# Start addresses of the weight products' operands, and the place of 256-column units in their ring slot

## The chip, the cores and the metric

The kernel runs on one core of a Trainium2 chip. The metric is the device time of one execution in microseconds (us). The engines named here are TensorE (PE; its weight loads are PEld), VectorE (DVE), ScalarE (ACT), GpSimd (POOL) and SyncE (SP, which here only issues loads and stores). SBUF is the on-chip memory of 128 partitions; an address below is a byte offset within a partition, the same in all partitions. PSUM is where PE writes its sums, in banks of 512 floats per partition.

## What is computed

Two transformer layers in a row on 256 tokens of width 1024, all in 32-bit floats. Cut to what matters:

```python
def first_block(x, ...):
    u = rms_norm(x, ln_pre_mix)
    proj = u @ w_in                       # 1024 -> 9232 columns
    q_a, k_a, v_a, qkv_b, z_b, b_b, a_b, gate_a, gate_b = split(proj)
    y_a = moba_attention(rope(q_a), rope(k_a), v_a)
    qkv_b = silu(causal_depthwise_conv(qkv_b, conv_w))
    y_b = rms_norm(gated_delta_rule(...)) * silu(z_b)
    merged = sigmoid(gate_a) * (y_a @ w_proj_a) + sigmoid(gate_b) * (y_b @ w_proj_b)
    h = x + rms_norm(merged @ w_out)
    f = rms_norm(h)
    h = h + rms_norm((silu(f @ w_ffn_gate) * (f @ w_ffn_up)) @ w_ffn_down)   # 2816 wide
    return h + sigmoid(h @ w_ple_gate) * rms_norm(p @ w_ple)

def second_block(x, mem, ...):
    mem_n = rmsnorm(mem)
    q, k, v, u = split(rmsnorm(x) @ w_in_2)
    mix = concat(diff_attention(q, k, v), causal_multiscale_pool(u) @ w_pool) @ w_out_2
    x = x + rmsnorm(mix)
    xq = rmsnorm(x) @ w_xq;  kv = mem_n @ w_xkv          # cross attention on mem
    x = x + rmsnorm(cross(xq, kv) @ w_xo)
    hf = rmsnorm(x)
    return x + rmsnorm((silu(hf @ w_gate) * (hf @ w_up)) @ w_down)           # 2816 wide
```

## The kernel before

**Split products.** Every weight product is made of three products of a rounded 32-bit type (fp32r): an operand x is held as xH, its rounded value, and xL, the rest, and x times w is xH wH + xH wL + xL wH. `split_mm` (lines 480 to 482) issues the three.

**Weight units.** All large weights pass through the chip in 294 units of 128 x 1024 floats. SP loads a unit into `raw`, a ring of 4 slots (line 448); ACT copies it rounded to `w_hi`, a ring of 6 slots (line 1192); POOL subtracts to make `w_lo`, also 6 slots, in two halves of 512 columns (line 469); PE then uses both. A unit is either rows of a wide matrix (128 rows by 1024 columns), or two or four blocks of 128 rows by 512 or 256 columns.

**Which operand is stationary.** `mm(dst, a, b)` loads a (128 columns) as the stationary operand and streams b as the moving one. In the trace's names the moving operand comes first: `L<-w_hi,uH` is weights moving over stationary uH.
- Column steps (`column_unit`) and row steps (`row_piece`): the activations are stationary, 512 columns of weights move. The stationary tile is uH/uL in nearly all steps, yH/yL in proj_a, hH/hL in the two down steps, mH/mL in xkv 2 and 3, pH/pL in the small ple product (`embed`). In the last ffn step (`("ffn", 1, 5)`, `("ffn", 2, 5)`) only 256 columns are left, so 256 columns of weights move.
- conv (lines 849 to 851) and `keys` (xkv 0 and 1, lines 739 to 741): 128 columns of weights are stationary, and the 256 tokens of uH/uL or of mH/mL move. Both have the same loops: over pairs of column tiles, the eight row blocks, and two tiles each. The small `ba` product (lines 822 to 824) has baH/baL, 16 columns, stationary, and uH/uL moving.

A conv or keys unit holds 24 products of 256 columns, a row or column unit 12 of 512.

**Order.** `SCHEDULE` lists the steps and each engine walks it in its own order with semaphores between. `w_lo_there` counts finished units, `w_used` units that PE has done with; ACT waits for `w_used` before it overwrites a slot, SP for `w_lo_there`. `FILLING` puts column units into gaps of the attention steps.

**Addresses.** `place` gives tiles out one after another and rounds sizes up to 32 bytes. The order is raw (16,384 bytes), w_hi and w_lo (24,576 each), uH and uL (8,192 each), table (1608 floats, 6,432 bytes), small (960 floats, 3,840 bytes), then from address Y on yH and yL, hH and hL at the same place, and from B on everything else, at whole or half KB from B (`big`). The first free byte of SBUF is 16,481.

Of the kernel before, what the change touches and what calls it, by code (L numbers as in the profile page):

```python
# [22 lines left out]
F32 = mybir.dt.float32  # L23
F32R = mybir.dt.float32r
# [5 lines left out]
P = 128  # L30
# [15 lines left out]
WINDOWS = (2, 4, 8, 16)  # L46
RAW, SPLIT = 4, 6
UNIT = 1024
KB = 1024
MAGIC = 1.5 * 2.0 ** 23  # L50
TWO_PI = (6.28125, 2029 / 2 ** 20, 2 * np.pi - 6.28125 - 2029 / 2 ** 20)
# [166 lines left out]
def build(nc, a, out, known):  # L218
# [4 lines left out]
    UNITS = weight_units(w)  # L223
# [7 lines left out]
    with ctx:  # L231
# [2 lines left out]


        base = -(-nc.sbuf_base // 32) * 32
        at = [base]

        def place(name, shape, dt=F32, offset=None):
            size = 4 * int(np.prod(shape[1:]))  # L240
            if offset is None:
                offset = at[0]
                at[0] += -(-size // 32) * 32
            return nc.alloc_sbuf_tensor_at(name, list(shape), dt, offset=offset)

        raw = place("raw", [P, RAW, UNIT])
        w_hi = place("w_hi", [P, SPLIT, UNIT], F32R)
        w_lo = place("w_lo", [P, SPLIT, UNIT], F32R)
        uH = place("uH", [P, KD, SEQ], F32R)
        uL = place("uL", [P, KD, SEQ], F32R)  # L250
        table = place("table", [P, 5 * P + 2 * NT * HD + ROPE2 + LEVELS * HALF])
        small = place("small", [P, 960])
        Y = at[0]
        yH = place("yH", [P, KD, SEQ], F32R)
        yL = place("yL", [P, KD, SEQ], F32R)
# [155 lines left out]
        w_hi_there, w_lo_there, w_used = sem("w_hi_there"), sem("w_lo_there"), sem("w_used")  # L411
# [51 lines left out]
        @block.gpsimd  # L463
        def _(pool):
            for n in range(len(UNITS)):
                pool.wait_ge(w_hi_there, n + 1)
                for half in range(2):
                    cc = slice(half * UNIT // 2, (half + 1) * UNIT // 2)
                    last = nc.gpsimd.tensor_tensor(w_lo[:, n % SPLIT, cc], raw[:, n % RAW, cc], w_hi[:, n % SPLIT, cc].bitcast(F32),  # L469
                                                   ALU.subtract)  # L470
                last.then_inc(w_lo_there, 1)

# [2 lines left out]
        def _(pe):  # L475
# [6 lines left out]
                return mm(dst, sL, wH, start=False, stop=stop)  # L482

            def unit(n, k):
                slot = n % SPLIT
                return (w_hi[:, slot, :].rearrange("p (k n) -> p k n", k=k),
                        w_lo[:, slot, :].rearrange("p (k n) -> p k n", k=k))

            def column_unit(step, j, banks, n=512, sH=uH, sL=uL, tiles=range(NT), ks=None):

# [316 lines left out]
            for step in SCHEDULE:  # L807
                kind = step[0]
                if kind == "u":
                    n = CONV * 24 + KD  # L810
# [7 lines left out]
                elif kind == "ba":  # L818

                    pe.wait_ge(*VE(("u",), "split"))  # L820
                    for k in range(KD):
                        mm(Q[0][0:16, 0:SEQ], baH[:, k, :], uH[:, k, :], start=k == 0, stop=False)
                        mm(Q[0][0:16, 0:SEQ], baH[:, k, :], uL[:, k, :], start=False, stop=False)
                        last = mm(Q[0][0:16, 0:SEQ], baL[:, k, :], uH[:, k, :], start=False, stop=k == KD - 1)
                    last.then_inc(*PE.mark(step))
                elif kind == "rates":
                    pe.wait_ge(*VE(("ba",), "turned"))
                    for t in range(NT):
                        last = turn(Q[1][:, t * 16:t * 16 + 16], baT[0:16, t * P:(t + 1) * P], ident[0:16, 0:16])
                    last.then_inc(*PE.mark(step))  # L830
                elif kind == "conv":
# [7 lines left out]
                    for pair in range(2):  # L839
                        for k in range(KD):  # L840
# [5 lines left out]
                            for ct in (pair, pair + 2):  # L846
# [4 lines left out]
                                last = mm(bank, sL, uH[:, k, :], start=False, stop=k == KD - 1)  # L851
                            if pair == 1 and k % 2 == 1:
                                last.then_inc(w_used, 1)
                elif kind == "tok":
                    gr = step[1]
                    for part in range(3):
                        for t in range(NT):
# [8 lines left out]
                            for i in range(GH):  # L866
                                last = turn(Q[b % 3][:, i * P:(i + 1) * P], C[:, part * GH + i, t * P:(t + 1) * P], ident)
# [3 lines left out]
                elif kind == "decay":  # L871
# [6 lines left out]
                    for t in range(NT):  # L878
                        last = mm(Q[3][:, t * 8:t * 8 + GH], tri, g[:, t * 8 + gr * GH:t * 8 + gr * GH + GH], start=True, stop=True)
# [6 lines left out]
                elif kind == "feat":  # L886
# [6 lines left out]
                    for b, (what, t) in enumerate(lots):  # L893
# [5 lines left out]
                        for i in range(GH):  # L899
                            last = turn(Q[b % 3][:, i * P:(i + 1) * P], src[what](t, i), ident)  # L900
# [4 lines left out]
                    for t in range(NT):  # L905
                        for i in range(GH):
                            last = mm(Q[2 * t + i // 2][:, (i % 2) * 256:(i % 2 + 1) * 256], kT[:, t, i, :],
                                      kbqT[:, t, i, :, :].rearrange("p a b -> p (a b)"), start=True, stop=True)
# [3 lines left out]
                elif kind == "att":  # L912
                    gr = step[1]
                    for b in range(4):
# [3 lines left out]
                        for i in range(2):  # L918
                            for t in range(NT):
                                last = turn(Q[b][:, i * SEQ + t * P:i * SEQ + (t + 1) * P], mtok[:, part, t, 2 * pair + i, :], ident)  # L920
# [3 lines left out]
                    for i in range(GH):  # L924
                        last = mm(Q[0][:, i * P:(i + 1) * P], qTa[:, i, 0:P], kTa[:, i, 0:P], start=True, stop=True)
                    last.then_inc(*PE.mark(step, "scores", 0))
                    for i in range(GH):
                        last = mm(Q[1 + i // 2][:, (i % 2) * SEQ:(i % 2 + 1) * SEQ], qTa[:, i, P:SEQ], kTa[:, i, :], start=True, stop=True)
# [4 lines left out]
                    for b, j in enumerate((0, 1, 2)):  # L933
# [3 lines left out]
                        for i in range(GH):  # L937
                            last = turn(Q[b][:, i * P:(i + 1) * P], pr[:, i, j * P:(j + 1) * P], ident)
# [4 lines left out]
                    for i in range(GH):  # L943
                        bank = Q[3 if i < 2 else 0]
                        c0 = (i % 2) * SEQ
                        mm(bank[:, c0:c0 + SEQ], mtok[:, 2, 0, i, :], prT[:, i, 0:SEQ], start=True, stop=False)
                        last = mm(bank[:, c0 + P:c0 + SEQ], mtok[:, 2, 1, i, :], prT[:, i, SEQ:3 * P], start=False, stop=True)
# [4 lines left out]
                elif kind == "inv":  # L952
# [18 lines left out]
                    for l in range(1, LEVELS):  # L971
                        A = [Q[2], Q[3], Q[0], Q[1]] if l % 2 else Q
                        top = l == LEVELS - 1
                        for t in range(NT):
                            pe.wait_ge(*(VE(step, "T", l - 1, t) if l > 1 else AC(step, "T", 0, t)))
                            for i in range(GH):
                                for b, d in enumerate(diagonal):
                                    if top and b == 0:
                                        continue
                                    k = diagonal[0] if top else d  # L980
                                    last = mm(tiles(A[t], i)[b], AT[k, t, i, d], T[k, t, i, :], start=True, stop=True)  # L981
# [5 lines left out]
                        for t in range(NT):  # L987
# [3 lines left out]
                            for i in range(GH):  # L991
                                if top:
                                    d = diagonal[1]
                                    last = mm(tiles(A[t], i)[0], X[d, t, i, :], TT[d, t, i, d], start=True, stop=True)
# [186 lines left out]
        def _(act):  # L1181
# [3 lines left out]
            def split_up_to(n):  # L1185

                while made[0] < min(n, len(UNITS)):
                    u = made[0]
                    act.wait_ge(w_landed[u % RAW], 16 * (u // RAW + 1))
                    if u >= SPLIT:  # L1190
                        act.wait_ge(w_used, u - SPLIT + 1)
                    copy(w_hi[:, u % SPLIT, :], raw[:, u % RAW, :]).then_inc(w_hi_there, 1)  # L1192
                    made[0] += 1

            def hi_wide(step, dst, tiles=range(4)):
# [1119 lines left out]
```

## Time and profile before

| | |
|---|---|
| median of 3 runs | 1032.4 us (1031.9 to 1032.85) |
| the profiled execution's own time | 1033.94 us |
| its span, first to last instruction | 1032.1 us |
| PE busy | 986.9 us (96%) |
| POOL busy | 738.5 us (72%) |
| ACT busy | 514.7 us (50%) |
| DVE busy | 368.2 us (36%) |
| mean granted TensorE clock | 0.997 |

The span is counted from the first to the last instruction; the time of the execution holds a little more, here 1.8 us. Busy times are the union of an engine's instructions. A product's duration runs from its start until its last result is out, and the next product starts while it still runs, so a row's duration is longer than the distance to the next start.

### The profile page before, as it was taken

The numbers are of one execution on the slowest core, as the hardware profiler recorded it, in microseconds if no ns is written. First come the engines' busy times: TensorE is split into PE (matmuls) and PEld (weight loads), VectorE is DVE, ScalarE is ACT, GpSimd is POOL, SyncE is SP. The second block draws the span as 40 slices with busy tenths as digits, with TensorE's granted clock in tenths as the row PEclk, the third lists the DMA queues.
The fourth block names the chain that finished last, engine by engine and source line by source line (L and its number), as shares of the span: only waits on it lengthen the run. The fifth ranks groups of instructions, "written<-read, shape, count | busy, mean of one in ns | idle before, by whom it ended". The sixth has DMA issues, their size and how long they took to land.

```text
span 1032.1 us, 15349 instructions
## 1 busy us (share of the span) xinstructions
PE 986.9 (96%) x6004; PEld 828.4 (80%) x6004; DVE 368.2 (36%) x864; ACT 514.7 (50%) x759; POOL 738.5 (72%) x592
## 2 busy tenths in 40 slices
PE   5989999999999998999999998999999989999997
PEld 4978888988888876788888876889868868888885
DVE  5676423676424235212112344243162161111103
ACT  5474624465624335555544455475465465444431
POOL 6767442776632777879986966878767469998881
PEclk9999999999999999999999999999999999999999
DMA  7545332555332665667665545654545247766551
GB/s 258 177 135 169 97 104 62 162 166 164 103 104 82 225 204 153 192 183 214 199 196 164 174 144 191 219 182 142 185 150 177 70 137 231 212 187 189 177 165 41
DMA packets 76752, 167.37 MB, mean 162 GB/s; under 512 B 8348, under 2 KB 13704, under 8 KB 76552
## 3 DMA queue, kind: packets, MB, share of 16 engines
q1 hardware_dynamic: 71296, 156.40, 49.3%
q10 hardware_dynamic: 5384, 9.99, 2.9%
q8 instruction: 47, 0.77, 0.3%
q14 instruction: 25, 0.20, 0.1%
HBM read 165.32 MB, written 1.05 MB: 161 GB/s over the span
## 4 chain that ended last, share of the span: by engine, by line
PE 75%; POOL 7%; DVE 7%; ACT 5%; DMA 3%; issue 2%; DVEq 0%; ACTq 0%
PE L L480 18%; PE L L482 17%; PE L L481 17%; POOL w_lo L469 7%; ACT w_hi L1192 2%; PE L L849 2%; PE L L851 2%; PE L L850 2%; DVE small L1741 1%; PE Q L981 1%; PE Q L963 1%; DMA raw<-in_w_in 1%; DMA raw<-in_w_ffn_gate 1%; PE Q L685 1%; PE Q L482 1%
## 5 line engine op out<-in xcount | busy, mean ns | idle before, releaser
L469 POOL TENSOR_TENSOR w_lo<-raw,w_hi 128x512 fp32r<-128x512 f32 x588 | 738.3, 1293 | 272.7 <-ACT w_hi L1192 272.1
L1192 ACT CAST w_hi<-raw 128x1024 fp32r<-128x1024 f32 x294 | 305.7, 1053 | 278.8 <-PE L L482 135.6
L480 PE MATMUL L<-w_hi,uH 128*128 128x512 f32 (+1 forms) x832 | 329.2, 396 | 13.6 <-POOL w_lo L469 5.0
L482 PE MATMUL L<-w_hi,uL 128*128 128x512 f32 (+1 forms) x832 | 318.7, 383 | 0.0
L481 PE MATMUL L<-w_lo,uH 128*128 128x512 f32 (+1 forms) x832 | 318.4, 383 | 0.0
L480 PEld LDWEIGHTS L<-w_hi,uH 128*128 128x128 f32 x832 | 156.8, 188 | 55.4 <-DVE uL L1772 10.6
L482 PEld LDWEIGHTS L<-w_hi,uL 128*128 128x128 f32 x832 | 156.9, 189 | 31.3
L481 PEld LDWEIGHTS L<-w_lo,uH 128*128 128x128 f32 x832 | 157.0, 189 | 27.5 <-issue 0.5
L480 PE MATMUL L<-w_hi,hH 128*128 128x512 f32 x176 | 70.2, 399 | 1.4 <-issue 1.4
L482 PE MATMUL L<-w_hi,hL 128*128 128x512 f32 x176 | 69.6, 395 | 0.0
L481 PE MATMUL L<-w_lo,hH 128*128 128x512 f32 x176 | 69.6, 395 | 0.0
L1735 DVE TENSOR_TENSOR hL<-Q,hH 128x512 fp32r<-128x512 f32 x22 | 15.2, 691 | 125.6 <-ACT hH L1596 125.2
L849 PE MATMUL L<-uH,w_hi 128*128 128x256 f32 x192 | 54.8, 286 | 1.1 <-DVE baH L1890 0.8
L1741 DVE TENSOR_SCALAR small<-small 128x1 f32<-128x1 f32 x201 | 45.5, 226 | 25.4 <-ACT xv L1522 13.4
L850 PE MATMUL L<-uL,w_hi 128*128 128x256 f32 x192 | 54.3, 283 | 0.0
L851 PE MATMUL L<-uH,w_lo 128*128 128x256 f32 x192 | 54.3, 283 | 0.0
L1806 DVE TENSOR_TENSOR L<-L,gA 128x512 f32<-128x512 f32 x20 | 14.0, 699 | 102.3 <-ACT hg L1279 101.8
L1744 DVE SCALAR_TENSOR_TENSOR hm<-L,small,sil 128x512 f32<-128x512 f32 (+1 forms) x24 | 17.0, 706 | 74.5 <-PE L L482 74.0
L480 PEld LDWEIGHTS L<-w_hi,hH 128*128 128x128 f32 x176 | 33.1, 188 | 9.4 <-issue 1.7
L482 PEld LDWEIGHTS L<-w_hi,hL 128*128 128x128 f32 x176 | 33.1, 188 | 8.0
L481 PEld LDWEIGHTS L<-w_lo,hH 128*128 128x128 f32 x176 | 33.1, 188 | 7.7
L849 PEld LDWEIGHTS L<-uH,w_hi 128*128 128x128 f32 x192 | 36.8, 192 | 1.6 <-DVE baH L1890 1.0
(327 smaller groups left out, 1157.1 us busy)
## 6 DMA issues: line engine op xcount, KB each, us to landing
raw<-in_w_in SPq DMA_DIRECT2D x88, 512.0 KB, 3.6
raw<-in_w_ffn_gate SPq DMA_DIRECT2D x22, 512.0 KB, 3.7
raw<-in_w_ffn_up SPq DMA_DIRECT2D x22, 512.0 KB, 3.6
raw<-in_w_ffn_down SPq DMA_DIRECT2D x22, 512.0 KB, 3.5
raw<-in_w_gate SPq DMA_DIRECT2D x22, 512.0 KB, 3.7
raw<-in_w_up SPq DMA_DIRECT2D x22, 512.0 KB, 3.6
raw<-in_w_down SPq DMA_DIRECT2D x22, 512.0 KB, 3.5
raw<-in_w_out SPq DMA_DIRECT2D x16, 512.0 KB, 4.2
```

Source lines behind the costliest of these rows:

```text
L469: last = nc.gpsimd.tensor_tensor(w_lo[:, n % SPLIT, cc], raw[:, n % RAW, cc], w_hi[:, n % SPLIT, cc].bitcast(F32), ALU.subtract)
L480: mm(dst, sH, wH, start=start, stop=False)
L481: mm(dst, sH, wL, start=False, stop=False)
L482: return mm(dst, sL, wH, start=False, stop=stop)
L849: mm(bank, sH, uH[:, k, :], start=k == 0, stop=False)
L850: mm(bank, sH, uL[:, k, :], start=False, stop=False)
L851: last = mm(bank, sL, uH[:, k, :], start=False, stop=k == KD - 1)
L1192: copy(w_hi[:, u % SPLIT, :], raw[:, u % RAW, :]).then_inc(w_hi_there, 1)
L1735: v(V.tensor_tensor(out_, x_, y_, op), *name)
L1741: v(V.tensor_scalar(out_, x_, s1, s2_, op0, op1), *name)
L1744: v(V.scalar_tensor_tensor(out=out_, in0=x_, scalar=s_, in1=y_, op0=op0, op1=op1), *name)
L1806: v(V.tensor_tensor(L[b][:], L[b][:], gA[:, c * 512:(c + 1) * 512], ALU.mult))
```

## The change

Two things. First, `base` and the address Y are rounded up to a multiple of 64 bytes instead of 32. Second, each slot of w_hi and w_lo becomes 16 floats longer (64 bytes, so slots stand 4160 bytes apart instead of 4096), and a function `split_half` gives the place of unit n in its slot: for the units of conv, of xkv 0 and 1, and of the last step of each ffn, it begins 8 floats (32 bytes) into the slot; for all others at its start. The ACT copy, the POOL subtraction and PE's views all go through `split_half`. The lengthened rings move everything behind them by 768 bytes.

```diff
         base = -(-nc.sbuf_base // 32) * 32
+        base = -(-base // 64) * 64
...
-        w_hi = place("w_hi", [P, SPLIT, UNIT], F32R)
-        w_lo = place("w_lo", [P, SPLIT, UNIT], F32R)
+        w_hi = place("w_hi", [P, SPLIT, UNIT + LINE], F32R)
+        w_lo = place("w_lo", [P, SPLIT, UNIT + LINE], F32R)
+
+        def split_half(ring, n, c0=0, c1=UNIT):
+
+
+            step = UNITS[n][0]
+            lead = LINE // 2 if step[0] in ("conv", "xkv") and step not in (("xkv", 2), ("xkv", 3)) or step in (("ffn", 1, 5), ("ffn", 2, 5)) else 0
+            return ring[:, n % SPLIT, lead + c0:lead + c1]
+
...
         small = place("small", [P, 960])
+        at[0] = -(-at[0] // 64) * 64
         Y = at[0]
...
-                    last = nc.gpsimd.tensor_tensor(w_lo[:, n % SPLIT, cc], raw[:, n % RAW, cc], w_hi[:, n % SPLIT, cc].bitcast(F32),
+                    last = nc.gpsimd.tensor_tensor(split_half(w_lo, n, cc.start, cc.stop), raw[:, n % RAW, cc],
+                                                   split_half(w_hi, n, cc.start, cc.stop).bitcast(F32),
                                                    ALU.subtract)
...
-                slot = n % SPLIT
-                return (w_hi[:, slot, :].rearrange("p (k n) -> p k n", k=k),
-                        w_lo[:, slot, :].rearrange("p (k n) -> p k n", k=k))
+                return (split_half(w_hi, n).rearrange("p (k n) -> p k n", k=k),
+                        split_half(w_lo, n).rearrange("p (k n) -> p k n", k=k))
...
-                    copy(w_hi[:, u % SPLIT, :], raw[:, u % RAW, :]).then_inc(w_hi_there, 1)
+                    copy(split_half(w_hi, u), raw[:, u % RAW, :]).then_inc(w_hi_there, 1)
```

`LINE` is 16.

## Rows read from the trace of the kernel before

**Rows 1.** The page: busy time by engine, and the chain that ended last, by engine.
```profile
PE 986.9 (96%) x6004; PEld 828.4 (80%) x6004; DVE 368.2 (36%) x864; ACT 514.7 (50%) x759; POOL 738.5 (72%) x592
...
PE 75%; POOL 7%; DVE 7%; ACT 5%; DMA 3%; issue 2%; DVEq 0%; ACTq 0%
```

**Rows 2.** Waits of PE: total us, times, longest.
```profile
PE L L480 <- POOL w_lo L469: 5.0, 12, 0.8
...
PE Q L867 <- ACT tok L1382: 3.1, 1, 3.1
```

**Rows 3.** Timeline of PE, an ffn step: start us, us, engine, line.
```profile
462.27 0.39 PE L481 MATMUL L<-w_lo,uH 128*128 128x512 f32 x1
...
483.61 0.39 PE L482 MATMUL L<-w_hi,uL 128*128 128x512 f32 x1
```

**Rows 4.** Timeline of PE, the second down step.
```profile
970.15 0.40 PE L482 MATMUL L<-w_hi,hL 128*128 128x512 f32 x1
...
1019.85 0.40 PE L482 MATMUL L<-w_hi,hL 128*128 128x512 f32 x1
```

**Rows 5.** Timeline of PE, xkv 2.
```profile
717.79 0.39 PE L480 MATMUL Q<-w_hi,mH 128*128 128x512 f32 x1
...
727.82 0.40 PE L481 MATMUL Q<-w_lo,mH 128*128 128x512 f32 x1
```

**Rows 6.** Timeline of PE, conv part 1 of the first group.
```profile
31.03 0.28 PE L851 MATMUL L<-uH,w_lo 128*128 128x256 f32 x1
...
41.95 0.28 PE L849 MATMUL L<-uH,w_hi 128*128 128x256 f32 x1
```

**Rows 7.** Timeline of PE, keys (xkv 0).
```profile
690.08 0.28 PE L740 MATMUL L<-mL,w_hi 128*128 128x256 f32 x1
...
699.41 0.28 PE L739 MATMUL L<-mH,w_hi 128*128 128x256 f32 x1
```

**Rows 8.** Timeline of PE, the last ffn step of the first layer.
```profile
518.29 0.28 PE L480 MATMUL L<-w_hi,uH 128*128 128x256 f32 x1
...
523.80 0.28 PE L481 MATMUL L<-w_lo,uH 128*128 128x256 f32 x1
```

**Rows 9.** Groups of PE by line and shape: count, busy us, mean ns, idle before.
```profile
L480 PE MATMUL L<-w_hi,uH 128*128 128x512 f32 x768 | 310.9, 405 | 13.6 <-POOL w_lo L469 5.0 <-DVE uL L1772 4.6 <-DVE small L1741 2.8
...
L480 PE MATMUL L<-w_hi,hH 128*128 128x512 f32 x176 | 70.2, 399 | 1.4 <-issue 1.4
...
L849 PE MATMUL L<-uH,w_hi 128*128 128x256 f32 x192 | 54.8, 286 | 1.1 <-DVE baH L1890 0.8 <-POOL w_lo L469 0.3
...
L480 PE MATMUL L<-w_hi,uH 128*128 128x256 f32 x64 | 18.3, 285 | 0.0
```

**Rows 10.** The ba product: timeline of PE, and the group of its weight load.
```profile
28.02 0.28 PE L822 MATMUL Q<-uH,baH 128*16 128x256 f32 x1
...
30.45 0.28 PE L822 MATMUL Q<-uH,baH 128*16 128x256 f32 x1
...
L822 PEld LDWEIGHTS Q<-uH,baH 128*16 128x16 f32 x8 | 0.8, 94 | 0.1
```

**Rows 11.** The chain that ended last, in order of time: start us, us, what.
```profile
783.30 0.87 PE Q L764 x8
...
810.24 3.57 PE Q L803 x32
```

**Rows 12.** Groups on POOL and DVE, columns as in rows 9.
```profile
L469 POOL TENSOR_TENSOR w_lo<-raw,w_hi 128x512 fp32r<-128x512 f32 x588 | 738.3, 1293 | 272.7 <-ACT w_hi L1192 272.1
...
L1772 DVE TENSOR_TENSOR uL<-Q,uH 128x512 fp32r<-128x512 f32 x28 | 19.3, 691 | 48.7 <-ACT uH L1204 48.6
...
L1735 DVE TENSOR_TENSOR hL<-Q,hH 128x512 fp32r<-128x512 f32 x22 | 15.2, 691 | 125.6 <-ACT hH L1596 125.2
```

**Rows 13.** Windows, PE: stretch, length, busy (count), clock, DMA share, GB/s.
```profile
463.00:484.00 21.00, 21.00 (x95) 1.00 0.72 207
```

**Rows 14.** Windows, PE, just behind its wait for tok; columns as in rows 13.
```profile
76.10:79.30 3.20, 3.20 (x9) 0.50 0.72 245
```

More of the change, by code:

```diff
@@ L48 @@
 UNIT = 1024
+LINE = 16
 KB = 1024
```

## Prediction

> **What bounds the kernel now.** I read the page's busy shares first, then who TensorE (PE) waits for, then the starts of single products. PE is busy 986.9 of 1032.1 us and the chain that ended last runs through it for 75% [rows 1]. It is idle for the other 45.2 us, and little of that is owed to a supplier of weights: POOL's low halves 5.0 us in 12 waits [rows 2]. So the time is a sum of distances between starts of products, and a change of address can only matter through those distances, or through the engines that write the moved tiles.
>
> The view to learn from is the timeline of PE, where one product's start stands above the next. A mean duration (399 ns for the products on hH [rows 9]) is of no use here, since products overlap; the distance of starts counts. I divide the time between a first and a last row by the intervals between them:
> - 512 columns, stationary uH or uL, moving weights (a column step of the ffn): 462.27 to 483.61 us, 94 intervals, **227.0 ns** [rows 3].
> - 512 columns, stationary hH or hL (the down step): 970.15 to 1019.85, 213 intervals, **233.3 ns** [rows 4].
> - The same with stationary mH or mL (xkv 2, a column step again): 717.79 to 727.82, 43 intervals, 233.3 ns [rows 5].
> - 256 columns, stationary weights, moving uH (conv): 31.03 to 41.95, 91 intervals, **120.0 ns** [rows 6].
> - 256 columns, stationary weights, moving mH (keys, the same loop nest): 690.08 to 699.41, 80 intervals, **116.6 ns** [rows 7].
> - 256 columns, stationary uH, moving weights (last ffn step): 518.29 to 523.80, 46 intervals, 119.8 ns [rows 8].
>
> Now the addresses, worked out from the code. The first free byte is 16,481; rounded to 32 or to 64 it is 16,512, a multiple of 64. raw, the rings, uH and uL have sizes that are multiples of 64, so before the change they all start at 0 past a multiple of 64. table has 1608 floats, 6432 bytes, 32 past one; small has 3840. So everything from Y on (yH, hH, mH, pH and all that `big` places) stands 32 past. All slices taken are multiples of 512 bytes. The two groups are then: 512 columns with both operands at 0, 227.0; stationary at 32, 233.3, in a row step and in a column step. 256 columns with both at 0, 120.0 and 119.8; moving at 32, 116.6. mH under a column loop takes 233.3 while uH under the same loop takes 227.0, and conv and keys have one loop nest, so the order of the loops does not explain it.
>
> **The change part by part.** No instruction is added or removed and no wait is moved. What moves is addresses.
>
> (1) Everything from Y on goes from 32 to 0. Products of 512 columns with a stationary operand there: 176 x 3 with hH [rows 9]; by the code, 8 units of proj_a and 8 of xkv 2 and 3 with 12 products each and 2 of ple with 12, 216 more; together 744. They become the pair 0 and 0 that uH has: 744 x (233.3 - 227.0) = 744 x 6.3 = **4.7 us** less.
>
> (2) The last ffn step's weights stand at 32, stationary uH at 0. That is the pair of the keys now (stationary 0, moving 32): 64 x 3 = 192 products, 192 x (119.8 - 116.6) = **0.6 us** less [rows 7 to 9].
>
> (3) conv: stationary weights at 32, moving uH at 0, 192 x 3 = 576 products [rows 9]. The trace of before has no full-width product of this pair at 256 columns. The nearest row is the ba product: stationary baH at 32, moving uH at 0, 28.02 to 30.45 us, 21 intervals, 115.7 ns; but baH is 16 columns wide, and loading it takes 94 ns [rows 10], less than the 120 of a product, so it may hide what a load of 128 columns would show. Bounds: the keys' 116.6 on one side; on the other, 512 columns lost 6.3 ns from this same pair, so 126.3. I take 116.6, since both 256-column rows with operands on different residues agree: 576 x 3.4 = **2.0 us** less (the other end: 3.6 us more).
>
> (4) keys (8 units of 24, 192 products): weights 0 to 32 and mH 32 to 0, the pair turned round. By (3) it stays at 116.6: 0; the other end is 126.3, 1.9 us more.
>
> (5) Other products with operands behind Y go from 32 and 32 to 0 and 0. The chain's rows give 3.57 us for 32 products of L803, both at 32, 112 ns each; the transposes of L764 with the identity at 0 and the other at 32 take 0.87 us for 8, 109 ns [rows 11]. So 3 ns on some 250 products of 128 columns, 0.75 us less, is one end; the 3.4 ns that the pair 0 and 0 costs at 256 columns, on some 350, 1.2 us more, is the other. I take 0.
>
> (6) The writers on other engines: DVE writes uL at 0 in 691 ns and hL at 32 in 691 [rows 12]. I take 0 for these, and the same for ACT. POOL never ran with a ring slot at 32 in this trace; its bound comes from slack: two halves of 1293 ns are 2.59 us for a unit [rows 12], a conv unit takes PE 24 x 120.0 = 2.88 us and would take 2.80, a 512-column unit 12 x 227.0 = 2.72. POOL would have to be 8% slower on conv units before PE noticed.
>
> Does a faster PE run into its supply? In the down steps the pace becomes 2.72 us a unit, the pace at which the ffn steps run already with PE busy 21.00 of 21.00 us at 207 GB/s [rows 13]. So the gain in (1) is not handed back to the DMA or to POOL. SP's load queue is held by POOL's low halves as before, with nothing moved in it.
>
> What lies beside other work: PE idles 3.1 us for ACT's copy of tok [rows 2], after conv part 2 of the first group and less than 2 us before the stretch of rows 14. What that part gains can end in this wait, since ACT's chain behind it starts from releases inside the part: at most its 96 products x 3.4 ns = 0.3 us, and I take 0.3 off. The wait is followed by 3.2 us at granted clock 0.50, that is 1.2 GHz [rows 14], which do 1.6 us of work. Should the idle time move so that this stretch goes, 1.6 us less; should a second one appear, 1.6 more.
>
> **Sum**: 4.7 + 0.6 + 2.0 - 0.3 = 7.0 us less. The profiled execution has a span of 1032.1 us and took 1033.94; the median of the runs is 1032.4, 0.15% below, so a difference carries over one to one: span 1025.1, time **1025.4**.
>
> **A rule that speaks against it.** The rows say that the address of one operand changes the distance by 3 to 6 ns. The Trainium skill, "TensorE: Matmul & The Clock Gate", Part 2, says that PE reads the moving operand and the next weights over two independent SBUF ports, so loading takes nothing from the running product, and its section "Back-to-back issue gap" gives N / 2.4 + 2.5 ns, about 216 and 109. By that page nothing here depends on a start address and the sum would be 0. The trace has 227 and 120, and 233.3 and 116.6 on another address, so it does not agree.
>
> **Rivals.**
> - *Only a misplaced stationary operand costs, at any width.* For it: 227.0 to 233.3 when the stationary one moves to 32. Then (1) and (2) stay, conv loses 576 x 6.3 = 3.6 and keys 192 x 9.7 = 1.9: 4.7 + 0.6 - 3.6 - 1.9 = -0.2, so 1032.6. Against: the ba row at 115.7, with its narrow load as the doubt. Chance 0.06.
> - *The stationary side is indifferent at 256 columns*: conv stays at 120.0, keys go to it (192 x 3.4 = 0.7 more). 4.7 + 0.6 - 0.7 - 0.2 = 4.4 less, 1028.0. Chance 0.09.
> - *Slower: the place within more than 64 bytes.* The ring slots go from 4096 to 4160 bytes apart, so their place within 128 bytes and above, against uH, now differs from slot to slot; before, every slot had the same. If odd slots then behave as other residues do at 512 columns, half of the 2304 products on uH (1152) come at 233.3: 7.3 us more, and half of (1) is lost, 2.4. Then 7.3 + 2.4 - 7.0 = 2.7 more, 1035.1. It decides from about 1,100 products that lose 6.3 ns. For it: no row before has a residue of 64. Against: slices of uH and of the ring already differ by many multiples of 512 bytes, and all come at 227 or 120. Chance 0.09.
> - *The address does nothing* and the slower steps share another cause: 1032.4. Against it stand the pairs with one loop nest. Chance 0.04. It is also what the page named above would have.
>
> **How the numbers follow.** The forecast, faster by 7.0 us, has 0.72. Its own ends: below, 1025.4 - 0.75 - 1.6 = 1023.0; above, the second rival's 1028.0 with 1.2 (5) and something of the clock's 1.6, 1030.1. The range 1023.0 to 1030.1 holds forecast and second rival, 0.81; the other three, 0.19, are left out. 0.2% is 2.1 us, about what a measurement of this kernel can tell from no change. Faster: 0.72 + 0.09 = 0.81. Same: 0.06 + 0.04 = 0.10. Slower: 0.09.
>
> **What the changed profile would show.** Starts of the down step 227 apart for 233.3 prove (1); conv at 116.6, 120 or 126 decides (3) between forecast, second and first rival; the last ffn step at 116.6 proves (2); the ffn steps on uH must stay at 227, and if they alternate by slot the third rival is right. POOL's mean must stay near 1293 and its idle time before L469 large. The prediction fails if the 512-column products on uH get slower, or if POOL on slots at 32 rises above 1.40 us a half.

## The result: 0.4% slower

The changed kernel took 1036.6 us (median of 5, 1036.36 to 1036.87) beside 1031.9 us for the kernel before (5 runs, 1030.77 to 1032.85): 4.7 us more by the medians, 0.45%; the ratio worked out over all runs is 1.0038, with a 95% interval of 1.0027 to 1.005. Measured again on another chip it was 1036.63 beside 1033.01, ratio 1.0029 (1.0018 to 1.0039). Forecast was 1025.4 with a range of 1023.0 to 1030.1, so size and sign were both wrong. The profiled execution of the changed kernel has a span of 1034.6 us and took 1036.44.

The page of the changed kernel, busy time by engine and the chain by engine (for [rows 1]), and its group on POOL (for [rows 12]):

```profile
PE 991.9 (96%) x6004; PEld 829.5 (80%) x6004; DVE 368.3 (36%) x864; ACT 514.4 (50%) x759; POOL 741.6 (72%) x592
...
PE 79%; DVE 7%; POOL 5%; ACT 5%; issue 2%; DMA 2%; DVEq 0%; ACTq 0%
...
L480 POOL TENSOR_TENSOR w_lo<-raw,w_hi 128x512 fp32r<-128x512 f32 x588 | 741.4, 1300 | 272.3 <-ACT w_hi L1203 271.9
```

The same 6004 products keep PE busy 5.0 us longer (986.9 before). POOL's half went from 1293 to 1300 ns and it still idles 272 us, so the ring slots cost it nothing that matters. PE's waits (columns as in [rows 2]) are no longer than before:

```profile
PE L L492 <- POOL w_lo L480: 4.5, 9, 0.8
...
PE Q L878 <- ACT tok L1393: 3.0, 1, 3.0
```

And the windows of PE (stretch, length, busy and count, clock, DMA share, GB/s) show the ffn and down stretches wholly busy at full clock, and the stretch of reduced clock in its old place.

```profile
463.00:484.00 21.00, 21.00 (x93) 1.00 0.72 210
972.00:1020.00 48.00, 48.00 (x209) 1.00 0.43 132
75.00:80.00 5.00, 5.00 (x20) 0.66 0.70 207
```

The same window of the kernel before, for the last of these rows (behind [rows 14]):

```profile
75.00:80.00 5.00, 5.00 (x21) 0.66 0.68 210
```

The time therefore lies again in the distances between starts. Timeline of PE in the changed kernel, first and last row of six stretches, in the order in which they run (conv, ffn, last ffn step, keys, xkv 2, down):

```profile
31.02 0.28 PE L862 MATMUL L<-uH,w_lo 128*128 128x256 f32 x1
...
40.98 0.28 PE L862 MATMUL L<-uH,w_lo 128*128 128x256 f32 x1
...
463.15 0.39 PE L494 MATMUL L<-w_hi,uL 128*128 128x512 f32 x1
...
483.70 0.39 PE L493 MATMUL L<-w_lo,uH 128*128 128x512 f32 x1
...
520.02 0.28 PE L493 MATMUL L<-w_lo,uH 128*128 128x256 f32 x1
...
525.34 0.28 PE L493 MATMUL L<-w_lo,uH 128*128 128x256 f32 x1
...
690.05 0.28 PE L750 MATMUL L<-mH,w_hi 128*128 128x256 f32 x1
...
699.48 0.28 PE L751 MATMUL L<-mL,w_hi 128*128 128x256 f32 x1
...
719.22 0.39 PE L493 MATMUL Q<-w_lo,mH 128*128 128x512 f32 x1
...
727.75 0.39 PE L494 MATMUL Q<-w_hi,mL 128*128 128x512 f32 x1
...
972.04 0.39 PE L492 MATMUL L<-w_hi,hH 128*128 128x512 f32 x1
...
1021.25 0.39 PE L492 MATMUL L<-w_hi,hH 128*128 128x512 f32 x1
```

With their 84, 89, 45, 79, 37 and 213 intervals these give 118.6, 230.9, 118.2, 119.4, 230.5 and 231.0 ns. The next table has the means over all undisturbed pairs of a class in both traces, and what the difference makes of those pairs. A pair is two recorded neighbours of the same class; it is undisturbed when its distance shows no wait, no missing record and no reduced clock. Of the 2304 products on uH and uL 2094 such pairs are left. Because this mean takes in the products just behind a break, it stands up to 1 ns above the distance in one smooth stretch (227.9 beside the 227.0 of [rows 3]).

| class | answers | pairs | before, ns | after, ns | us |
|---|---|---|---|---|---|
| 512 columns on uH, uL (ffn) | rows 3 | 2094 | 227.9 | 231.1 | +6.7 |
| 512 columns on hH, mH, pH, yH | rows 4, 5 | 719 | 233.1 | 230.9 | -1.6 |
| conv | rows 6 | 557 | 119.9 | 118.95 | -0.55 |
| keys | rows 7 | 186 | 117.0 | 119.1 | +0.4 |
| last ffn step | rows 8 | 186 | 119.9 | 118.2 | -0.3 |

The sum is +4.65 us, close to the difference of the medians (+4.7) and to that of PE's busy time (+5.0). The two profiled spans differ by 2.5 only: the profiled execution of the kernel before was 2.0 us above the later median, and PE was idle for 45.2 us in it beside 42.7. So the loss is found: it lies in the products that were fast, and which the change was said to leave alone.

### The profile page after: what moved, and what is told of

It reads as the page before. It is cut to its first block, busy times and chain, and to the rows that moved or that the text cites. A ratio compares the mean times of both kernels' runs of the same rounds, so it can differ in the third digit from the quotient of the medians.

```text
span 1034.6 us, 15349 instructions
## 1 busy us (share of the span) xinstructions
PE 991.9 (96%) x6004; PEld 829.5 (80%) x6004; DVE 368.3 (36%) x864; ACT 514.4 (50%) x759; POOL 741.6 (72%) x592
## 4 chain that ended last, share of the span: by engine, by line
PE 79%; DVE 7%; POOL 5%; ACT 5%; issue 2%; DMA 2%; DVEq 0%; ACTq 0%
PE L L492 19%; PE L L494 18%; PE L L493 18%; POOL w_lo L480 5%; PE L L860 2%; PE L L862 2%; ACT w_hi L1203 2%; PE L L861 2%; DVE small L1752 1%; PE Q L992 1%; PE Q L974 1%; DMA raw<-in_w_in 1%; PE Q L696 1%; PE Q L494 1%; PE Q L492 1%
```

## The experiments

The address facts, worked out from the code, now as a place **within 256 bytes**: before, w_hi, w_lo and uH begin at 128, and all slots and slices step by multiples of 512, so every product of the ffn has both operands on the same place. Y begins at 160, 32 past. After the change a ring is 6 x 4160 = 24,960 bytes, which isn't a multiple of 256: w_hi and uH begin at 128, w_lo at 0, Y at 192, and each slot is 64 further than the one before.

The prediction's theory is that the place within 64 bytes counts. The rival, grown out of the third one, is that a longer period counts, and that the slots and the displaced w_lo make the loss. The first four kernels separate them. Edits are made on the kernel before unless the text says otherwise. Each ratio is worked out over all runs on one chip, so it isn't exactly the ratio of the two medians.

**Y alone to 64 bytes** (e1_align).

```diff
         small = place("small", [P, 960])
+        at[0] = -(-at[0] // 64) * 64
         Y = at[0]
```

> The kernel before with Y rounded up to 64 bytes and nothing else; rings stay 4096 bytes a slot. Theory A (the address residue within 64 bytes is what counts, as long as every ring slot stands at the same residue within 512 bytes): the down step, proj_a, ple and xkv 2 and 3 come at 227 ns instead of 233.3, 744 x 6.3 = 4.7 us less, and the keys go to 120.0, 0.7 us more: about 4.0 us less than before, 1027.9 beside 1031.9. Theory B (the old spacings were owed to where these tiles stood and have nothing to do with 64 bytes): the 512-column products stay at 233 or go to 231, no more than 1.7 us less.

Measured: 1032.29 beside 1032.99, ratio 0.9998 (0.9987 to 1.001). The down step, timeline of PE:

```profile
970.06 0.39 PE L482 MATMUL L<-w_lo,hH 128*128 128x512 f32 x1
...
1017.89 0.40 PE L483 MATMUL L<-w_hi,hL 128*128 128x512 f32 x1
```

205 intervals, 233.3 ns, as in [rows 4]; the keys keep their distance as well (116.7, where the 64-byte theory has 120.0). Y now stands on a multiple of 64, 64 off the others within 256, and nothing is won. This one part of the change should have brought 4.7 us by step (1), and brought none. The 64-byte theory falls here.

**Slots 4160 apart, nothing else** (e2_stride). 128 spare bytes behind each ring keep w_lo and uH on the place of w_hi; slices become `[0:UNIT]`.

```diff
-        w_hi = place("w_hi", [P, SPLIT, UNIT], F32R)
-        w_lo = place("w_lo", [P, SPLIT, UNIT], F32R)
+        w_hi = place("w_hi", [P, SPLIT, UNIT + 16], F32R)
+        at[0] += 128
+        w_lo = place("w_lo", [P, SPLIT, UNIT + 16], F32R)
+        at[0] += 128
```

> The kernel before with the ring slots 4160 bytes apart instead of 4096; w_lo and uH are padded so that their starts keep their residues within 512 bytes, and Y keeps 32. Theory A (steps of 64 bytes between slots spoil it): products of 512 columns on uH go from 227 to about 231, 2304 x 4 = 9 us more, those on hH from 233.3 to about 231, 1.5 us less: 1039. Theory C (the spoiling is done inside a unit, by w_lo standing elsewhere within 512 bytes than w_hi, and not by the slots): only the first product of a unit can differ, so 227.0 stays to within 0.3 ns and the time stays at 1031.9.

Measured: 1038.21, ratio 1.0065 (1.0039 to 1.0092). One of its seven executions took 1048.79 and lifts the ratio; by the medians the kernel takes 5.2 us more, 0.5%. That execution is the profiled one. Its excess lies near the start, where PE waits 7.8 us for baL and the clock is then at half for 10.2 us; distances from there aren't counted. An ffn step, timeline of PE:

```profile
473.64 0.39 PE L483 MATMUL L<-w_lo,uH 128*128 128x512 f32 x1
...
495.41 0.40 PE L484 MATMUL L<-w_hi,uL 128*128 128x512 f32 x1
```

94 intervals, 231.6 ns. Over all undisturbed pairs the products on uH have 231.1 ns, on hH 233.6, conv 118.4, keys 118.5, last ffn step 118.8. The stride alone makes the products on uH as slow as in the changed kernel.

**w_lo displaced, slots as before** (e3_lo_off).

```diff
         w_hi = place("w_hi", [P, SPLIT, UNIT], F32R)
+        at[0] += 384
         w_lo = place("w_lo", [P, SPLIT, UNIT], F32R)
+        at[0] += 128
```

> The kernel before with w_lo 384 bytes further within 512, as in the changed kernel; slots stay 4096 apart, uH and Y keep their residues. Theory C (w_hi and w_lo at different places within 512 bytes): products of 512 columns on uH go to about 231, some 9 us more, 1040. Theory A (only slots or 64-byte residues): 227.0 stays, 1031.9.

Measured: 1039.33, ratio 1.0067 (1.0051 to 1.0082). Timeline of PE in an ffn step, six neighbours and the end of the stretch:

```profile
470.07 0.40 PE L483 MATMUL L<-w_lo,uH 128*128 128x512 f32 x1
470.30 0.39 PE L484 MATMUL L<-w_hi,uL 128*128 128x512 f32 x1
470.53 0.40 PE L482 MATMUL L<-w_hi,uH 128*128 128x512 f32 x1
470.77 0.40 PE L483 MATMUL L<-w_lo,uH 128*128 128x512 f32 x1
471.00 0.39 PE L484 MATMUL L<-w_hi,uL 128*128 128x512 f32 x1
471.23 0.40 PE L482 MATMUL L<-w_hi,uH 128*128 128x512 f32 x1
...
483.83 0.40 PE L482 MATMUL L<-w_hi,uH 128*128 128x512 f32 x1
```

From the first to the last row 59 intervals, 233.2 ns, and in the trace's finer starts distances of about 234, 230 and 236 that repeat with the three products of a group (over all products on uH 231.9). Only one product in three has its moving operand off by 128, yet all three are longer: the distance isn't a property of the product alone. So each of the two displacements in the change suffices for the loss, and they don't add up.

**uH and uL 256 bytes further** (e4_u_off), to see whether the period is 256 or 512. `at[0] += 256` stands ahead of uH and again behind uL, so that everything after them keeps its place within 512.

> The kernel before with uH and uL 256 bytes further within 512, as the changed kernel has them against w_hi; all else keeps its residue. Theory D (a fixed distance between moving and stationary operand within 512 bytes decides, as 32 against 0 did): products of 512 columns on uH leave 227 and conv leaves 120.0, all to one new steady value. Theories A and C: 227.0 and 120.0 stay, 1031.9.

Measured: 1032.18, ratio 0.9992 (0.9983 to 1.0001). Timeline of PE, an ffn step:

```profile
462.19 0.39 PE L483 MATMUL L<-w_lo,uH 128*128 128x512 f32 x1
...
479.87 0.39 PE L483 MATMUL L<-w_lo,uH 128*128 128x512 f32 x1
```

78 intervals, 226.7 ns; conv stays at 119.9. A displacement of 256 does nothing, while one of 128 costs (w_lo in e3) and one of 64 is no better than one of 32 (Y in e1, 233.3): a period of 256 bytes fits all of this. e8 below tests 128 once more.

In this expectation and the later ones "theory E" is the one that has come out so far: the places of the two operands within 256 bytes, relative to each other, decide.

**The changed kernel without its 32-byte lead** (e5_no_lead), the edit on the changed kernel: `lead = 0` in `split_half`.

> The changed kernel with no unit moved 32 bytes into its slot; slots stay 4160 bytes apart and w_lo 128 bytes off w_hi within 256. Theory E: products of 256 columns stay at 117 to 119 since slots and w_lo differ within 256 bytes anyway, so the time is that of the changed kernel within 1.5 us. If it is the 32 bytes that bring 256 columns below 120: conv back at 120.0, 1 to 2 us more than the changed kernel.

Measured: 1034.73 beside 1033.09, ratio 1.0029 (1.0008 to 1.0051). Conv 117.2, keys 117.0, last ffn step 117.3, where the changed kernel has 118.95, 119.1 and 118.2; products on uH stay at 231.0. Inside the changed kernel, with slots on changing places, the lead makes the 256-column products longer by 1 to 2 ns. That is 1.6 us by the distances, against the sign of the prediction's steps (2) and (3). By the medians the kernel without the lead is 1.9 us faster than the changed one, but these two were not timed on one chip. Its ratio of 1.0029 is lifted by one execution of 1045.12 among ten; by the medians it is 1.0016.

If the period is 256, step (1) of the prediction should work with the right number. Two kernels place Y alone, on the kernel before.

**Y on the rings' place within 256** (e7_y256), and **128 past it** (e8_y128).

```diff
         small = place("small", [P, 960])
+        at[0] += (base + 0 - at[0]) % 256
         Y = at[0]
```

In the second of them 0 is 128.

> The kernel before with Y moved on so that yH, hH, mH and pH stand at the same place within 256 bytes as uH and the ring slots; rings untouched. Theory E (512 columns come at 226.7 ns when moving and stationary operand stand at the same place within 256 bytes and this holds from product to product, and at 231 to 235 otherwise; 256 columns come at 120.0 in the first case and at 116 to 119 otherwise): the down step, proj_a, ple and xkv 2 and 3 go from 233.3 to 226.7, 744 x 6.6 = 4.9 us less, the keys from 116.6 to 120.0, 0.7 more: 4.2 us less than the kernel before. Theory B (these steps are slow for another reason): 233.3 and no change, as when Y was rounded to 64 bytes.

> As the run before, but Y 128 bytes away from the common place within 256. Theory E with a period of 256: the down step stays at 231 to 235 ns, the keys at 116 to 119; time as the kernel before within 1 us. With a period of 128: the down step at 226.7, the keys at 120.0, 4.2 us less.

Measured for the first: 1028.83 beside 1033.09, ratio 0.9968 (0.9956 to 0.9979); for the second: 1032.28, ratio 0.9991 (0.9982 to 1.0). The down step in the first, timeline of PE:

```profile
970.18 0.39 PE L481 MATMUL L<-w_hi,hH 128*128 128x512 f32 x1
...
1014.84 0.39 PE L483 MATMUL L<-w_hi,hL 128*128 128x512 f32 x1
```

and in the second:

```profile
970.16 0.40 PE L483 MATMUL L<-w_hi,hL 128*128 128x512 f32 x1
...
1014.78 0.39 PE L483 MATMUL L<-w_hi,hL 128*128 128x512 f32 x1
```

197 intervals of 226.7 ns against 192 of 232.4. 744 x 6.5 ns is 4.8 us; the keys, now on equal places too, go from 117.0 to 119.8 and give 0.5 back; 4.3 is left, and 4.3 was measured. In the second kernel both operands stand at a multiple of 64, and its down step stays slow; the 0.8 us between its median and the other has an interval that reaches a ratio of 1.0. So 128 is no period either.

**A sweep over places** (p1_probe): the previous kernel e7 with groups of 24 products appended behind the last output. Stationary slices of uH and uL, moving slices of one ring slot, one operand moved by 16 or 32 bytes from group to group. These products are extra work and their sums are read by nobody, so the kernel's own time, 1272.68 us, says nothing; only the distances inside the groups count.

```diff
+            def probe(n, moving, stationary, low=0, count=24):
+                for i in range(count):
+                    k, part = i // 3 % 2, i % 3
+                    w = w_lo if part == 1 else w_hi
+                    c = moving + (low if part == 1 else 0)
+                    u = uL if part == 2 else uH
+                    k0 = (i // 3 % 8) * SEQ + stationary
+                    mm(Q[0][:, 0:n], u[:].rearrange("p a b -> p (a b)")[:, k0:k0 + P], w[:, 0, k * 256 + c:k * 256 + c + n], start=i == 0, stop=i == count - 1)
```

> The run with Y at the common place within 256 bytes, with a sweep of products behind the last output, whose sums nobody reads; its time is longer by the sweep, some 250 us, and only the distances of starts in the sweep count. Each group is 24 products (xH wH, xH wL, xL wH in turn, as in the kernel) at one pair of places: moving operand shifted by 0 to 240 bytes in steps of 16, or stationary operand by 32 to 224 in steps of 32, at 512 and at 256 columns, and w_lo alone shifted at 512 columns. Theory E: 512 columns at 226.7 ns for no shift, 231 to 235 for every other; 256 columns at 120.0 for no shift, 116.7 for the moving operand at 32, between 113 and 119 elsewhere. If only the last 64 bytes counted (the theory of the prediction): shifts of 64, 128 and 192 read as no shift.

Timeline of PE, first and last row of four groups: 512 columns on equal places, the moving operand 64 and then 192 bytes further, and 256 columns with the stationary operand 64 further.

```profile
1038.26 0.39 PE L1189 MATMUL Q<-w_hi,uH 128*128 128x512 f32 x1
...
1043.48 0.39 PE L1189 MATMUL Q<-w_hi,uL 128*128 128x512 f32 x1
...
1060.46 0.39 PE L1189 MATMUL Q<-w_hi,uH 128*128 128x512 f32 x1
...
1065.73 0.39 PE L1189 MATMUL Q<-w_hi,uL 128*128 128x512 f32 x1
...
1105.06 0.39 PE L1189 MATMUL Q<-w_hi,uH 128*128 128x512 f32 x1
...
1110.42 0.39 PE L1189 MATMUL Q<-w_hi,uL 128*128 128x512 f32 x1
...
1214.56 0.28 PE L1189 MATMUL Q<-w_hi,uH 128*128 128x256 f32 x1
...
1217.17 0.28 PE L1189 MATMUL Q<-w_hi,uL 128*128 128x256 f32 x1
```

23 intervals each: 227.0, 229.1, 233.0 and 113.5 ns. All groups, by the bytes that one operand stands further than the other (the stationary one in steps of 32 only). An entry is the mean in ns of the last 18 distances of a group, since the first five still settle; over all 23 the means differ from it by up to 0.6 ns. Each group ran once, in one execution.

| bytes | 512, moving | 512, stationary | 256, moving | 256, stationary |
|---|---|---|---|---|
| 0 | 226.7 | | 120.0 | |
| 16 | 231.3 | | 118.6 | |
| 32 | 233.2 | 233.3 | 116.9 | 118.2 |
| 48 | 233.3 | | 118.4 | |
| 64 | 228.9 | 233.3 | 117.8 | 113.3 |
| 80 | 231.1 | | 119.9 | |
| 96 | 233.4 | 234.1 | 120.0 | 120.0 |
| 112 | 231.1 | | 113.3 | |
| 128 | 232.5 | 233.3 | 118.4 | 118.6 |
| 144 | 233.3 | | 118.7 | |
| 160 | 234.3 | 233.3 | 117.3 | 120.0 |
| 176 | 233.3 | | 119.3 | |
| 192 | 233.3 | 228.9 | 113.3 | 117.8 |
| 208 | 234.6 | | 119.6 | |
| 224 | 233.3 | 233.3 | 118.6 | 117.8 |
| 240 | 226.7 | | 116.9 | |

At 512 columns 0 is the best place, and the moving operand 64 ahead reads as the stationary one 192 ahead (228.9 both), and 192 ahead as the stationary one 64 ahead (233.3 both). So the difference of the two places is what counts, at 512 columns throughout. At 256 columns 0 is among the worst and some places give 113.3. With the low product's weights alone moved by 32 to 224 bytes all groups had 229.4 to 233.3. The sweep agrees with the kernel's own stages at the pairs that both have: 226.7, 120.0, 116.9 for the moving operand at 32, and 233.3 for the stationary one at 32 ([rows 3], [rows 6], [rows 7], [rows 4]). Two entries were not expected: at 512 columns a moving operand 240 further costs nothing, and one 64 further only 2.2 ns.

**The changed kernel with 256 in place of 64** (e9_full256), on the changed kernel: slots 4352 bytes apart, Y on the common place, the 32-byte lead kept, and small tiles of up to 32 columns moved into the gaps between slots, since room was short.

```diff
-LINE = 16
+LINE = 64
...
-        at[0] = -(-at[0] // 64) * 64
+        at[0] += (base - at[0]) % 256
```

> The changed kernel with slots 4352 bytes apart (256 more than 4096, not 64) and Y at the common place within 256 bytes; conv, keys and last ffn units keep their 32 bytes. The room comes from small tiles that are placed in the gaps between slots. Theory E: all 512-column products at 226.7 ns, conv, keys and the last ffn step at 116.7: 744 x 6.6 = 4.9, conv 576 x 3.3 = 1.9 and 192 x 3.3 = 0.6, 7.4 us less than the kernel before. If a stationary operand at 32 costs at 256 columns as at 512 (the first rival of the prediction): conv and keys at 126, some 0.2 us more in all than the kernel before.

Measured: 1027.0 beside 1033.09, ratio 0.9947 (0.9932 to 0.9963). The 512-column classes have means of 226.7 to 227.9 (uH as before), the last ffn step at 116.7, keys 118.35, conv 118.3:

```profile
31.04 0.28 PE L872 MATMUL L<-uH,w_lo 128*128 128x256 f32 x1
...
40.98 0.28 PE L872 MATMUL L<-uH,w_lo 128*128 128x256 f32 x1
```

84 intervals, 118.3 ns, which is what the sweep has for a stationary operand 32 further (118.2). By classes: 744 x 6.4 = 4.8, conv 576 x 1.6 = 0.9, last ffn step 192 x 3.2 = 0.6, keys 0.3 back: 6.0, and 6.1 was measured. Expected were 7.4, with 116.7 for conv and keys; a stationary operand 32 further doesn't give that. So the prediction's steps (1) and (2) hold once 256 takes the place of 64, and (3) holds at half its size.

**The same with the leads that the sweep has as best** (e10_best): 64 bytes for conv and keys, 112 for the last ffn steps.

```diff
-            lead = 8 if step[0] in ("conv", "xkv") and step not in (("xkv", 2), ("xkv", 3)) or step in (("ffn", 1, 5), ("ffn", 2, 5)) else 0
+            lead = 28 if step in (("ffn", 1, 5), ("ffn", 2, 5)) else 16 if step[0] == "conv" or step in (("xkv", 0), ("xkv", 1)) else 0
```

> Slots 4352 bytes apart and Y at the common place within 256, as in the run with all at the common place, but conv and keys units stand 64 bytes into their slot and the last ffn units 112, the two places at which the sweep read 113.3 ns. Theory E with the sweep's table: 512 columns at 226.7, conv, keys and last ffn step at 113.3. Against the kernel before 744 x 6.5 = 4.8, conv 576 x 6.6 = 3.8, keys 192 x 3.6 = 0.7, last ffn step 192 x 6.6 = 1.3, 10.6 us less in all, a ratio of 0.990. If the table of the sweep doesn't carry over to the kernel's own stream (other work beside it, units that change slots): 256 columns at 117 to 119, 6 to 7 us less.

Measured: 1023.72 beside 1033.01, ratio 0.9904 (0.9889 to 0.9919), the fastest of all: it beats both kernels. Timeline of PE, conv of the first group, conv of the second group, and the down step:

```profile
31.05 0.28 PE L872 MATMUL L<-uH,w_lo 128*128 128x256 f32 x1
...
40.00 0.28 PE L870 MATMUL L<-uH,w_hi 128*128 128x256 f32 x1
...
180.05 0.28 PE L870 MATMUL L<-uH,w_hi 128*128 128x256 f32 x1
...
200.07 0.28 PE L872 MATMUL L<-uH,w_lo 128*128 128x256 f32 x1
...
970.21 0.39 PE L502 MATMUL L<-w_hi,hH 128*128 128x512 f32 x1
...
1009.87 0.39 PE L503 MATMUL L<-w_lo,hH 128*128 128x512 f32 x1
```

79 intervals of 113.3 ns, 170 of 117.8, 175 of 226.6. The first conv stretch has what the sweep promised; the other has the same places and the same loop nest and doesn't. The trace shows where the distance changes. Six conv units (22.0 to 41.0 us) run at 113.3, then two small products stand between, and every conv unit behind them runs at 117.8:

```profile
40.91 0.28 PE L872 MATMUL L<-uH,w_lo 128*128 128x256 f32 x1
41.11 0.30 PE L850 MATMUL Q<-table,baT 16*128 16x16 f32 x2
41.34 0.39 PE L870 MATMUL L<-uH,w_hi 128*128 128x256 f32 x1
```

The keys do the reverse: 117.8 in the six units up to 702.7 us, then four small products, then 113.3 in the last two. In both cases the distance changed where other products had broken the stream, though not every such break changes it (the ba product stands between the second and the third of the six units). What picks one of the two is not shown. Over conv the mean is 116.5, over keys 116.7, over the last ffn steps 114.2. By classes: 744 x 6.6 = 4.9, conv 576 x 3.4 = 2.0, last ffn step 192 x 5.7 = 1.1, together 8.0. PE's busy time is 979.0 us, 7.9 less than before, which agrees. The medians differ by 9.3, and the interval of the ratio is 8.4 to 11.5 us; the 1.3 us that remain are not explained. Expected were 10.6 with 113.3 everywhere, or 6 to 7 if the sweep's table didn't carry over; it carried over in part.

**The changed kernel again**, on the chip of the kernel above (a2_after).

> The changed kernel once more, beside the run above on one chip. Theory E by the spacings read from both profiles: 512 columns on uH from 227.9 to 231.1, 2094 pairs, 6.7 us more; 719 on hH, yH, mH and pH 2.2 ns shorter, 1.6 less; conv 1.0 shorter, 0.5 less; keys 2.1 longer, 0.4 more; last ffn step 1.7 shorter, 0.3 less: 4.7 us more than the kernel before, a ratio of 1.0045. If the first comparison was chance, the ratio is within 0.2% of 1.

Measured: 1036.63 beside 1033.01, as given at the start. The loss is no matter of one chip.

## Why the prediction was wrong, point by point

**What bounds the kernel** held. The result is a sum of distances between starts; PE's waits for POOL and ACT went from 5.0 and 3.1 us to 4.5 and 3.0 and had no part in it. The cover that step (6) named for POOL held (1300 ns a half against a bound of 1.40 us a half).

**The step that failed is "Now the addresses".** It reduced every address to its place within 64 bytes. Before the change only two relations occurred, equal places and 32 apart, and these look the same whether one reckons within 64, 128 or 256 bytes. The rows allowed each of these; the text took the one that the change itself uses. It had the fact that should have stopped it, that all slices are multiples of 512 bytes, and used it against the third rival: slices that differ by many multiples of 512 said nothing about steps of 64. e1 refutes 64 with one line of code, e4 shows that a step of 256 changes nothing, and e7 against e8 shows the gain at the right place and a slow down step 128 off it.

What that did to each term:
- The term that isn't in the sum at all, the 2304 products on uH: taken to stay at 227, they went to 231.1, +6.7 us over the recorded pairs, more than the whole forecast gain. e2 shows the slots to suffice for it, e3 the displaced w_lo.
- Step (1), -4.7: hH, mH, pH and yH went from 233.1 to 230.9 and not to 227, -1.6. They came onto a varying relation, like all products of 512 columns. With Y on the right place the term is what the step said: e7, 226.7 ns.
- Step (2), -0.6: 119.9 to 118.2, -0.3. Its mechanism (stationary 0, moving 32, so 116.6) is right once the slots keep their place: 116.7 in e9.
- Step (3), -2.0: 119.9 to 118.95, -0.55. Here the pair itself was mis-sized too. With only the conv weights moved by 32 within 256 it reads 118.3 (e9) and not 116.6; the ba row at 115.7, with its narrow weights, was no measure for it. With the slots right the term is 576 x 1.6 = 0.9 less: the sign held, the size was double.
- Step (4), 0: keys went from 117.0 to 119.1, +0.4.
- Step (5), 0: right. The 1875 distances below 250 ns between the other products add up to 137.0 us before and 137.2 in the changed kernel. The rows that the step compared don't move either (transposes of cq with the identity 109.1 ns before and 109.0 after, products of xv and cpT 113.3 and 113.2), and in e7, where the same tiles come to equal places, the sum is 137.0 again. So the 112 against 109 ns of the step's two rows belonged to the kind of product and not to its address, and what the runs show on addresses holds for the split products alone.
- The wait for tok and the stretch at reduced clock: both still there, in the same place, and they decide nothing.

**The rivals.** The third came closest, with 1035.1 beside 1036.6: the place within more than 64 bytes, and slots as its cause, with "the 512-column products on uH get slower" named as what would make the prediction fail. It had a chance of only 0.09, and two of its parts were off. It had half of the products at 233.3 and half at 227, where all of them are mixed around 231, and it didn't see that a ring of 24,960 bytes also takes w_lo off the place of w_hi by 128. Its price of 7.3 us and the 6.7 found agree because 2304 x 3.2 is nearly 1152 x 6.3, which is chance. The first two gave 1032.6 and 1028.0 and had the wrong period in common with the forecast; with the right one, e9 speaks against both, since its conv, with a stationary operand 32 further, is 1.6 ns faster than at equal places, neither slower nor the same. *The address does nothing* is refuted by e7.

**The page named in the prediction.** The runs show that the place of one operand relative to the other is worth up to 8 ns in 227 at 512 columns and up to 6.7 in 120 at 256. The Trainium skill, "TensorE: Matmul & The Clock Gate", Part 2, has two independent read ports, so that a weight load takes nothing from the running product; distances that change with the place of the stationary operand alone (226.7 to 233.3 in the sweep) don't agree with that. Its section "Back-to-back issue gap", from which the prediction took 216 and 109, calls that formula the gap of a single isolated product and has about 131 ns at 512 columns for a stream of loads and products; the shortest mean distance at 512 columns in these runs is 226.7, so the trace agrees with neither. "SBUF — State Buffer", section "Operand start alignment", says of itself that it is about legality and not speed; all placements here lie within what it allows, and they differ in time by 1.5% (1023.7 to 1039.3).

**What stays open.** Why the two operands' relation within 256 bytes matters. That both streams read the memory at the same time and meet or miss each other is consistent with the difference of places as the variable, with the cost that spills over to neighbours in e3, and with the two distances at one placement in e10; none of the runs shows it. Also open are what picks one of the two distances in e10, and its 1.3 us.

## What to carry to other kernels

When a distance depends on an address, list which residues occur in the trace and at what period they could be told apart; the premise is only as fine as the differences that occur, and a change that brings a new difference (here a slot stride of 64 past a multiple of 4096) leaves what was measured. Then check every array behind the edit, since a ring that grows by an odd number of lines shifts all that follow. Where PE is the bound and its products come back to back, place the moving and the stationary operand of fp32r products with 512 columns alike within 256 bytes, keep slots at multiples of 256, and try other places for those of 256 columns: here that was worth 0.9 to 1.0% (e10), with PE's 6004 products and every other engine's count unchanged. The places for 256 columns are the less certain part, since one placement ran at two distances.

## What was unexpected of the hardware

- For fp32r products the period is 256 bytes; the other products don't react to the moves made here (137.0 to 137.2 us in all). At 512 columns equal places give 226.7 ns, a difference of 240 gives 226.7 too, 64 (moving, or 192 stationary) 228.9, and the rest 231.1 to 234.6.
- At 256 columns it is the other way round: equal places are among the slowest (120.0), and 113.3 occurs with the stationary operand 64 or the moving one 112 or 192 further. By difference alone this width reads less cleanly: moving 160 has 117.3 and stationary 96, the same difference, 120.0.
- One placement can have two steady distances: in e10 conv and keys run at 113.3 in some stretches and at 117.8 in others, unchanged from unit to unit until other products come between. The sweep has one group of 24 products for each place and couldn't show this; a place measured once is not yet a price.
- In the down step of the changed kernel the mean over the 12 products of a unit runs 229.8, 231.2, 231.1, 231.7, 230.8, 232.0 ns and then repeats, with a period of six units, which is the number of ring slots; in the kernel before nearly every group of 12 in an ffn step has 226.7, except those behind a wait.
